# Near scores in blocks of 32, squares in column groups, one gather sooner, the first unit in halves, a tail with four squares

## What is computed

```
def hgrn2_scan(q, logf, k, v, S0):
    ...
        b = jnp.cumsum(lfc, axis=2)
        diff = b[:, :, :, None, :] - b[:, :, None, :, :]
        decay = jnp.exp(jnp.where(causal, diff, -jnp.inf))
        scores = jnp.einsum('bhtk,bhtsk,bhsk->bhts', qc, decay, kc)
        o = (jnp.einsum('bhts,bhsv->bhtv', scores, vc)
             + jnp.einsum('bhtk,bhkv->bhtv', qc * jnp.exp(b), S))
...
def mixer(h, S0, buf, start_pos, lb, w_in, w_o, hg_norm, w_pool, pool_scale):
    proj = h @ w_in
    q, fx, ix, g, u = jnp.split(proj, [HG_WIDTH, 2 * HG_WIDTH, 3 * HG_WIDTH, 4 * HG_WIDTH], axis=-1)
    ...
def trunk(...):
    for l in range(DEPTH):
        h = rmsnorm(x, norm_mix[l])
        y, S, b = mixer(h, S_in[l], buf_in[l], start_pos, lbs[l], w_in[l], w_o[l], hg_norm[l], pool_w[l], pool_scale[l])
        x = x + y
        h = rmsnorm(x, norm_ffn[l])
        x = x + (swiglu(h, ...) if l % 2 == 0 else moe(h, ...))
    return rmsnorm(x, norm_final), jnp.stack(S_out), jnp.stack(buf_out)
```

## Time and profile before

| what | value |
|---|---|
| median of 3 runs | 851.43 us (851.15 to 852.05) |
| the profiled execution | 850.92 us |
| its span, first to last instruction | 849.0 us |
| mean granted TensorE clock | 0.996 |
| PE busy | 832.6 us (98%) |
| DVE / ACT / POOL busy | 681.3 (80%) / 574.1 (68%) / 169.5 us (20%) |
| HBM read | 214.25 MB |

### The profile page before, as it was taken

One profiled execution on the slowest core, in us unless ns is written; L12 is line 12 of the kernel. 1 busy time (PEld: TensorE's weight loads), 2 busy tenths in 40 slices (PEclk: granted clock), 3 DMA queues, 4 the chain that ended last, 5 costly groups with the idle time before them and its releaser, 6 DMA issues.

```text
span 849.0 us, 14351 instructions
## 1 busy us (share of the span) xinstructions
PE 832.6 (98%) x5471; PEld 726.6 (86%) x5471; DVE 681.3 (80%) x837; ACT 574.1 (68%) x715; POOL 169.5 (20%) x147
## 2 busy tenths in 40 slices
PE   6999999999999999999999999999999999999996
PEld 6999999999999999999988777777777777777776
DVE  5899678777665547996888889898998989898964
ACT  6857765544544348577966878787878787787842
POOL 4430276555411132303800000000000000000001
PEclk9999999999999999999999999999999999999998
DMA  8843267555678526424495999999999999899911
GB/s 301 313 159 108 78 236 253 186 185 173 245 276 274 194 100 209 139 100 176 161 310 177 384 381 421 322 408 338 395 376 355 391 344 414 320 422 323 395 66 52
DMA packets 52404, 222.01 MB, mean 262 GB/s; under 512 B 6208, under 2 KB 6336, under 8 KB 51694
## 3 DMA queue, kind: packets, MB, share of 16 engines
q1 hardware_dynamic: 50670, 209.61, 67.4%
q0 software_dynamic: 960, 9.50, 3.0%
q10 hardware_dynamic: 720, 2.18, 0.6%
HBM read 214.25 MB, written 7.47 MB: 261 GB/s over the span
## 4 chain that ended last, share of the span: by engine, by line
PE 93%; DVE 3%; ACT 2%; issue 1%; DMA 1%; DVEq 0%; ACTq 0%
PE bank L1812 43%; PE bank L1498 12%; PE bank L1499 12%; PE bank L1500 12%; PE bank L1656 2%; PE bank L1523 2%; PE bank L1868 2%; PE bank L1784 1%; PE bank L1821 1%; DVE sb_w_lo L997 1%; ACT sb_w_hi L570 1%; DMA sb_raw<-in_in_units_dram 1%; PE bank L1581 0%; PE bank L1749 0%; PE bank L1648 0%
## 5 line engine op out<-in xcount | busy, mean ns | idle before, releaser
L997 DVE TENSOR_TENSOR sb_w_lo<-sb_raw,sb_w_hi 128x1024 fp32r<-128x1024 f32 (+1 forms) x116 | 173.6, 1497 | 61.7 <-ACT sb_w_hi L570 60.5
L1498 PE MATMUL bank<-at_act_hi,sb_w_hi 128*128 128x264 f32 x672 | 194.1, 289 | 8.1 <-DVE sb_w_lo L997 8.1
L570 ACT ACTIVATE sb_w_hi<-sb_raw 128x1024 fp32r<-128x1024 f32 (+1 forms) x116 | 127.1, 1101 | 96.0 <-PE bank L1500 94.0
L1499 PE MATMUL bank<-at_act_lo,sb_w_hi 128*128 128x264 f32 x672 | 191.5, 285 | 0.0
L1500 PE MATMUL bank<-at_act_hi,sb_w_lo 128*128 128x264 f32 x672 | 191.3, 285 | 0.0
L1812 PE MATMUL bank<-sb_w_hi,at_packed 128*96 128x512 f32 (+1 forms) x768 | 189.7, 375 | 0.2 <-DVE at_packed L1264 0.2
L1044 DVE TENSOR_TENSOR sb_w_lo<-at_raw_e,sb_w_hi 128x1408 fp32r<-128x1408 f32 (+1 forms) x112 | 159.7, 1447 | 27.0 <-ACT sb_w_hi L638 26.4
L638 ACT ACTIVATE sb_w_hi<-at_raw_e 128x1408 fp32r<-128x1408 f32 (+1 forms) x112 | 139.0, 1242 | 38.2 <-PE bank L1812 38.2
L1044 DVE TENSOR_TENSOR sb_w_lo<-sb_raw,sb_w_hi 128x1408 fp32r<-128x1408 f32 (+1 forms) x104 | 149.8, 1479 | 14.3 <-ACT sb_w_hi L638 14.3
L1812 PEld LDWEIGHTS bank<-sb_w_hi,at_packed 128*96 128x96 f32 x768 | 122.4, 161 | 38.1 <-DVE at_packed L1264 0.6
L638 ACT ACTIVATE sb_w_hi<-sb_raw 128x1408 fp32r<-128x1408 f32 (+1 forms) x104 | 130.3, 1259 | 32.7 <-PE bank L1812 32.5
(11 more groups left out here) (275 smaller groups left out, 1255.7 us busy)
## 6 DMA issues: line engine op xcount, KB each, us to landing
sb_raw<-in_moe_w_up_dram SPq DMA_DIRECT2D x36, 704.0 KB, 7.2
at_raw_e<-in_moe_w_down_dram SPq DMA_DIRECT2D x49, 512.0 KB, 7.0
at_raw_e<-in_moe_w_gate_dram SPq DMA_DIRECT2D x35, 704.0 KB, 9.2
sb_raw<-in_up_units_dram SPq DMA_DIRECT2D x44, 512.0 KB, 3.3
sb_raw<-in_moe_w_gate_dram SPq DMA_DIRECT2D x29, 704.0 KB, 9.2
sb_raw<-in_in_units_dram SPq DMA_DIRECT2D x39, 512.0 KB, 3.8
sb_raw<-in_moe_w_down_dram SPq DMA_DIRECT2D x39, 512.0 KB, 5.2
at_raw_e<-in_moe_w_up_dram SPq DMA_DIRECT2D x28, 704.0 KB, 6.2
```

Of the source, the lines that this page charges most:

```text
L570: act.activation(w_hi[s][:, 0:kts, :], raw[s][:, 0:kts, :], ACT.Copy).then_inc(hi_done, 1)
L997: dve.tensor_tensor(w_lo[s][:, 0:kts, :], raw[s][:, 0:kts, :], w_hi[s][:, 0:kts, :].bitcast(f32), ALU.subtract).then_inc(lo_done, 1)
L1498: pe.matmul(out[:, 0:T], w_hi[s][:, k, :], hi[:, c, :], start=(c == 0), stop=False)
L1499: pe.matmul(out[:, 0:T], w_hi[s][:, k, :], lo[:, c, :], start=False, stop=False)
```

## The change

**Near scores.** Scores 0 to 6 of a layer reach at most 32 tokens, so only the four blocks of 32x32 on the diagonal of each 128x128 matrix are made. `score` now issues 16 matmuls (four heads by four blocks), each with 32 stationary and 32 moving columns, block b in the PE's column group at 32b and in the bank's partitions 32b to 32b+31. The masks are 32 wide (constants shrink by 768 columns), `take` and `part_scores` work on 128x128 instead of 128x512, and write a new tile `near` with three parts (two segments and `both`). ACT's new `put_near` copies the four blocks of a segment from `near` into `scores`, behind `put(5)` for segment 0 and behind `put(6)` for segment 1; PE waits for five puts a layer.

**First unit.** ACT's queue loads unit 0 in two halves; ACT and DVE split it half by half, and PE begins with the first.

**Routing.** The eight square sums take 32 stationary columns each, in turn in the four column groups, all ahead of the routing's matmuls. ACT copies the 128x264 result scaled by 1/32 (`sums_m`), three 88x1 matmuls sum over the partitions and turn; ACT takes the root on 88x3. The transposes L1844 and the copy L1326 go.

**Gathers.** Three stand ahead of the first unit and the later pairs one earlier; their banks are 4, 6, 5 instead of 4, 6, 7. DVE's `rest_of_packed(2)` stands ahead of `mark_slots(4, 8)`.

**Tail.** POOL adds tiles 1 to 4 only; PE sums tiles 0, 5, 6, 7. DVE scales tiles 0 to 2, 3 to 6 and 7 behind the adds of tiles 5, 6 and 7.

Three semaphores of the gates become one; the path for more than 96 tokens of an expert, which these inputs do not take, is adapted.

```diff
-C_CORR = C_MASK + 128 * (1 + len(LEVELS))
+C_CORR = C_MASK + NEAR * (MARKED + 3)
...
-        both = at("both", [128, HEADS, SEG], 81024)
+        near = at("near", [128, 3, HEADS, NEAR], 81024)
+        both = near[:, 2, :, :]
...
-        GATHERS = {j: (2 * j + 2, 2 * j + 3) for j in range(-1, KT - 1)}
+        GATHERS = {-1: (0, 1, 2)} | {j: (2 * j + 3, 2 * j + 4) for j in range(KT - 2)} | {KT - 2: (2 * KT - 1,)}
...
-            return (4, 6, 7)[n % 3]
+            return (4, 6, 5)[n % 3]
...
-            for kt in range(1, KT - 2):
+            for kt in range(1, KT - 3):
                 gp.wait_ge(tail_squared, kt + 1)
...
-            act.dma_start(raw[0][:, 0:KT, :], unit_source("in0", 0, 0)).then_inc(raw_full[0], 16)
+            act.dma_start(raw[0][:, 0:KT // 2, :], unit_source("in0", 0, 0)[:, 0:KT // 2, :]).then_inc(first_in, 16)
+            act.dma_start(raw[0][:, KT // 2:KT, :], unit_source("in0", 0, 0)[:, KT // 2:KT, :]).then_inc(raw_full[0], 16)
...
-                    split(0, 0, 0, kts, guard=False)
-                    for kt in range(2, KT):
+                    act.wait_ge(first_in, 16)
+                    act.activation(w_hi[0][:, 0:KT // 2, :], raw[0][:, 0:KT // 2, :], ACT.Copy).then_inc(first_hi, 1)
+                    for kt in range(2, KT // 2):
+                        scale_x(0, kt)
+                    act.wait_ge(raw_full[0], 16)
+                    act.activation(w_hi[0][:, KT // 2:KT, :], raw[0][:, KT // 2:KT, :], ACT.Copy).then_inc(hi_done, 1)
+                    for kt in range(KT // 2, KT):
                         scale_x(0, kt)
...
                         put(PUTS[(it, s)])
+                        if PUTS[(it, s)] < len(LEVELS):
+                            put_near(PUTS[(it, s)] - MARKED)
...
+                def put_near(seg):
+
+                    act.wait_ge(scores_zeroed, 2 * (L + 1))
+                    for b in range(SEG // NEAR):
+                        block = slice(NEAR * b, NEAR * (b + 1))
+                        done = act.activation(scores[block, seg, :, block], near[block, seg, :, :], ACT.Copy)
+                    done.then_inc(scores_put, 1)
...
+            act.wait_ge(summed, 4)
+            act.activation(sums_m[:, :], bank[3][:, 0:T], ACT.Copy, scale=1.0 / 32).then_inc(plain_rounded, 1)
...
-                    src = bank[score_bank(i)][:, :].rearrange("p (h t) -> p h t", h=HEADS)
+                    src = bank[score_bank(i)][:, 0:HEADS * NEAR].rearrange("p (h t) -> p h t", h=HEADS)
...
-                    dst = scores[:, i, :, :] if i < 2 else both[:, :, :]
-                    dve.copy_predicated(dst, mask(max(i - 1, 0)), src).then_inc(scores_taken, 1)
+                    dve.copy_predicated(near[:, min(i, 2), :, :], mask(max(i - 1, 0)), src).then_inc(scores_taken, 1)
...
-            for kt in range(KT):
-                scale_f(kt)
+                for k in {5: (0, 1, 2), 6: (3, 4, 5, 6), 7: (7,)}.get(kt, ()):
+                    scale_f(k)
...
                     for h in range(HEADS):
-                        mm = pe.matmul(bank[score_bank(i)][:, 128 * h:128 * (h + 1)], left(h), right(h), start=True, stop=True)
+                        if i >= MARKED + 2:
+                            mm = pe.matmul(bank[score_bank(i)][:, 128 * h:128 * (h + 1)], left(h, slice(0, SEG)), right(h, slice(0, SEG)), start=True, stop=True)
+                            continue
+                        for b in range(SEG // NEAR):
+                            block = slice(NEAR * b, NEAR * (b + 1))
+                            mm = pe.matmul(bank[score_bank(i)][block, NEAR * h:NEAR * (h + 1)], left(h, block), right(h, block), start=True, stop=True,
+                                           tile_position=(0, block.start))
...
-                pe.wait_ge(scores_put, 3 * (L + 1))
+                pe.wait_ge(scores_put, 5 * (L + 1))
...
-            sum_m(range(2))
+            for kt in range(KT):
+                pe.wait_ge(x_squared, KT // 2 + (1 if kt < KT - 1 else 2))
+                rows = slice(32 * (kt % 4), 32 * (kt % 4 + 1))
+                mm = pe.matmul(bank[3][rows, 0:T], ones[:, 0:32], square_m[:, kt, :], start=(kt < 4), stop=(kt >= 4), skip_group_check=True,
+                               tile_position=(0, rows.start))
+            mm.then_inc(summed, 1)
...
+            pe.wait_ge(plain_rounded, 3)
+            for i, (t0, rows) in enumerate(TOKEN_TILES):
+                mm = pe.matmul(bank[3][0:rows, i:i + 1], sums_m[:, t0:t0 + rows], ones[:, 0:1], start=True, stop=True)
+            mm.then_inc(summed, 1)
...
-            pe.wait_ge(tail_summed, KT - 3)
-            for kt in (0, KT - 2, KT - 1):
+            pe.wait_ge(tail_summed, KT - 4)
+            for kt in (0, KT - 3, KT - 2, KT - 1):
```

116 lines of the change are left out of this document (60 added, 56 removed).

## The result

The changed kernel takes **854.70 us** (median of 11 runs, 851.37 to 856.64), the kernel before beside it 851.34 (11 runs, 850.29 to 852.05). The ratio over all runs is 1.0032, with an interval of 1.0024 to 1.0041 (the two medians alone give 1.0039). The prediction was 847.0 (844.6 to 851.8), faster. Its sign was wrong, and the time lies outside its range.

The account below looks back on a forecast made before the run. The prediction took PE, busy 98% of the span, to bound the kernel. Its terms -2.1 (to v of layer 0), -1.9 (layer 1), -0.2 (routing) and -0.2 (tail) sum to -4.4, 847.0 us, range 844.6 to 851.8.

Parts of the forecast that it names:

- PE's saving in the score loop arrives if DVE saves as much: Score loop: PE's 3.5 us a layer counts only if DVE, busy 17.50 of 17.50 us, saves as much.
- the start's -0.8: First unit in halves: PE begins near 6.2 instead of 8.09; -0.8 us is left behind the square sum (0 to -1.1).
- Behind it PE is busy, the difference stays: Behind v of layer 0: the -2.1 us gained up to there stays through the feed-forward.
- the forecast was -2.1: Up to v of layer 0: start and seven calls bring the chain 4.3 us earlier, copies lengthen it 2.24; -2.1 us.
- Near calls on PE: Near score calls: each takes PE 0.5 us instead of 1.0, seven a layer, -3.5 us a layer on PE.
- records have a floor: Rival, near score calls: small matmuls start no closer than 28 ns, a call stays 1.0 us; +2.6, 854.0 us; chance 0.13.
- Takes: DVE's masked copies of near scores: 0.22 us each (0.15 to 0.35) instead of 0.74, 0.5 less for each of seven.
- Copies on ScalarE: Eight added ACT copies a layer, in the chain to v: 2.24 us a layer (1.6 to 2.56).
- The routing's term, -0.2: Routing: PE saves some 2.5 us, but first gather and ninth unit wait for others; -0.2 us (-0.8 to +0.6).
- Tail: -0.2 forecast: Tail: PE starts 0.6 us earlier with four POOL adds but sums 0.47 longer; -0.2 us (-0.5 to +0.2).
- DVE keeps the loop: Rival, score loop: masked takes cost 0.47 us, DVE saves only 0.25 a call, PE waits; -0.9, 850.5 us; chance 0.16.
- The sign that was named for this: Score loop: PE waiting for DVE's sides in every unit would show the forecast wrong; no size given.

Follow-up runs that it names:

- the copies on GpSimd: The changed kernel with a layer's eight near copies moved from ACT to GpSimd: 847.48 us, ratio 0.9962 to the kernel before.
- the near part alone: The kernel before with only the near scores in 32x32 blocks added, copies on ScalarE; start, routing and tail as before: 852.86 us, ratio 1.002.
- v filled in both places: The changed kernel with 14 idle matmuls ahead of v in layer 0 and three ahead of PE's wait in the routing: 852.29 us, ratio 1.0009.
- without the near part: The changed kernel with the scores as in the kernel before; new start, routing, gathers and tail stay: 851.46 us, ratio 1.0009.
- the start alone: The kernel before with only the first unit in halves and the merged semaphores: 851.26 us, ratio 1.0005.
- the two kernels with copies on GpSimd and the first unit whole: The changed kernel with near copies on GpSimd and the first unit undivided: 847.24 us; the same with two idle matmuls in the routing: 846.69 us.

## Why the prediction was wrong

Three steps failed: that PE's saving in the score loop arrives if DVE saves as much, the start's -0.8, and "Behind it PE is busy, the difference stays". Up to v of layer 0 the forecast was -2.1 and the profile has +1.1; of the difference the loop carries 1.2, the start 1.6 (half of its +0.8 is luck, above), the copies 0.3. Behind v two falls of the clock cost 2.3 and 3.1 in this execution.

**Near calls on PE: right.** 0.46 to 0.49 us each, 0.5 forecast. Two calls that follow each other:

```profile
344.38 0.46 PE L1562 MATMUL bank<-at_proj,at_keys 128*32 128x32 f32 x32
344.65 0.49 PE L1562 MATMUL bank<-at_proj,at_mirrored_keys 128*32 128x32 f32 x32
```

The second begins 0.27 behind the first, so 32 records start 8 ns apart; the bar of 0.46 also holds the last record's own 0.2. The rival *records have a floor* is out, and with it, for column groups, the 25 ns that the Trainium skill gives ("TensorE: Matmul & The Clock Gate", section "Wait — 56ns, not 53.3ns?"): here the measurement decides.

**Takes: sized within their bounds, and worth nothing in the loop.** They take 0.28 to 0.29 (0.22 forecast, 0.15 to 0.35). The first step that failed is the sentence that PE's saving arrives if DVE saves as much, with DVE busy 17.50 of 17.50. The 17.50 was no sum of DVE's work: the split that lasts 1.21 alone stands in it once at 1.67 and three times at 2.19 to 2.26, for half a microsecond and then a whole one of standing behind GpSimd. The length of one instruction beside its other occurrences would have told it. Relative to the first score call, the chain in layer 0 begins 2.30 sooner, where 3.5 was forecast: 0.63 of it ahead of the ring, nothing in the three distances of the ring (4.52, 4.47, 4.44 before; 4.53, 4.47, 4.44 after), 0.83 behind it, and 0.85 in `part_scores`. In layer 1 it begins 2.83 sooner, where 3.8 was forecast.

**Copies on ScalarE: the size within its bounds, 2.54 for 2.24 (1.6 to 2.56).** That they stand in the chain to v was right too. v of layer 0 comes 0.28 later in the stage where -1.3 was forecast (-2.1 with the start), v of layer 1 0.21 sooner where -1.9 was. With the call's saving cut to 2.3 by the ring, 2.54 of copies is more than it. With the copies on GpSimd v of layer 0 comes 2.06 sooner than before, near the -2.1 that was forecast; that is luck, since neither the start nor the loop gave what the forecast added up.

**The start: -0.8 forecast, nothing measured.** Alone it is +0.1 between the medians, and the ratio's interval leaves out -0.8. The first half load was not the trouble, it was used at 5.43. The second half, at 7.84, was: the forecast left ACT's squares 0.6 sooner, and they came 0.9 later.

**The clock: not in the prediction at all.** It foresaw that PE would wait 2.6 us at v, and gave this wait no price behind v. The wait was 3.81, and from inside it the clock stood at half for 6.83 us. From v to the first score call of layer 1 this costs 2.3 (258.16 us against 255.83; the near part alone 258.50, with v filled in both places 255.94). The routing's term, -0.2, is what the kernels without a fall show (v of layer 1 to the first expert unit: 46.93 before, 46.62 to 46.82 with the copies on GpSimd or without the near part), but saving 2.5 us of matmuls there left the clock to fall in a part of the runs. With the fall the time from the first gather to the end is 422.4, against 419.3 with the copies on GpSimd and no fall.

**Tail: -0.2 forecast, and right where the clock holds.** In the kernel without the near part PE's last sums begin 0.6 sooner after the scatter, as forecast, and last 0.5 longer, as forecast; the matmuls behind them take 1.58 instead of 1.26, and the clock falls at 842.24, just there, so the tail is 0.2 longer than before. Every profile has a fall in the tail, 1.5 to 4.6 us behind the scatter. Where it comes at the end of those matmuls or behind them (they take 0.90 to 0.92), the way from the scatter's end to the end of the span is 9.12 and 9.16 with the old tail (the near part alone, the start alone) and 8.96 and 8.97 with the new one (the two kernels with copies on GpSimd and the first unit whole).

**The rivals.** *DVE keeps the loop* had the place right and the mechanism wrong: it said that the takes would cost too much, while what kept the loop was GpSimd's hold on DVE, at each price of a take that was measured (0.73, 0.28 and 0.16). The sign that was named for this, a wait of PE for DVE's sides in every unit, was not there: in layer 0 PE ran ahead and met the chain only at v. None of the cases had a fall of the clock.

## What to carry to other kernels

Before work is saved in a loop in which an engine is busy all the time, compare its instructions there with the same ones elsewhere: one that is longer there may be waiting inside its own bar, as the split was here, and then the engine that it waits for can set the pace. And a saving on TensorE that another chain cannot follow is no gain that is merely lost: it turns into a wait, and a wait or a thin stretch can cost the clock as well, so move the chain (here the copies, to an idle engine) or leave the matmuls where they are. In a kernel whose runs spread, read the granted clock of each run before explaining the median.
